# Output-projection weights ahead of the residual stream, its scaling on ScalarE, and modulation tiles spread 3, 2, 3, 2, 3, 2, 1, 0 over the mix stage of a hybrid mLSTM/Fourier diffusion step

## What is computed

```python
mod = silu(c) @ w_mod + b_mod                 # 6 x 1024 per token group
sh1, sc1, g1, sh2, sc2, g2 = split(mod, 6)
h = x * (1 + sc1) + sh1
...
merged = sigmoid(ga) * y_a + sigmoid(gb) * y_b
out = merged @ w_out
x = layer_norm(ALPHA * x + g1 * out, ln_gain[0], ln_bias[0])
h2 = x * (1 + sc2) + sh2
a, u = split(h2 @ w_ffn_in, 2)
f = (silu(a) * u) @ w_ffn_out
x = layer_norm(ALPHA * x + g2 * f, ln_gain[1], ln_bias[1])
```

## Time and profile before

| | |
|---|---|
| median of 3 runs | 1492.03 us (1490.08 to 1495.1) |
| the profiled execution | 1492.6 us, its span 1490.8 us |
| mean granted TensorE clock | 0.987 of full speed |
| PE busy | 1420.3 us (95%) |
| DVE busy | 886.2 us (59%) |
| POOL busy | 807.2 us (54%) |
| ACT busy | 329.6 us (22%) |

### The profile page before, as it was taken

The page is one execution under the profiler, slowest core; times in us unless marked ns, Lnnn a source line. Parts: engine busy times, 40 slices in busy tenths (PEclk is TensorE's granted clock), DMA queues, the critical chain, the costliest instruction groups (busy, mean ns, idle before and its releaser), DMA issues. The chain is left out here.

```text
span 1490.8 us, 24040 instructions
## 1 busy us (share of the span) xinstructions
PE 1420.3 (95%) x9397; PEld 1390.5 (93%) x9397; DVE 886.2 (59%) x1306; ACT 329.6 (22%) x563; POOL 807.2 (54%) x352
## 2 busy tenths in 40 slices
PE   5999989999999999999999999899999999999993
PEld 5999988999989989989999999899999999999993
DVE  7576786246626724753673889878997665611114
ACT  4452322221122122122233000232221111100002
POOL 1165566642463354255246777566767766756552
PEclk9999999999999999999999999899999999999997
DMA  8524244321421331132055445222223222241211
GB/s 330 193 95 146 89 168 168 104 71 61 134 73 47 99 105 57 51 134 80 31 187 203 144 167 209 91 71 69 71 70 141 70 73 82 70 177 64 78 63 70
DMA packets 57236, 164.29 MB, mean 110 GB/s; under 512 B 6072, under 2 KB 20544, under 8 KB 55880
## 3 DMA queue, kind: packets, MB, share of 16 engines
q1 hardware_dynamic: 40760, 150.87, 29.3%
q10 hardware_dynamic: 16400, 12.30, 2.5%
HBM read 145.81 MB, written 17.33 MB: 109 GB/s over the span
## 5 line engine op out<-in xcount | busy, mean ns | idle before, releaser
L676 POOL TENSOR_TENSOR w_hi<-raw,zero 128x1024 fp32r<-128x1024 f32 x156 | 313.8, 2012 | 590.9 <-PE psum L753 448.2
L680 POOL TENSOR_TENSOR w_lo<-raw,w_hi 128x1024 fp32r<-128x1024 f32 x164 | 436.6, 2662 | 38.9 <-ACT w_hi L1248 26.6
L753 PE MATMUL psum<-h_hi,w_hi 128*128 128x256 f32 (+1 forms) x768 | 177.8, 313 | 11.7 <-POOL w_lo L680 11.3
L753 PE MATMUL psum<-h_lo,w_hi 128*128 128x256 f32 (+1 forms) x768 | 176.2, 311 | 0.0
L753 PE MATMUL psum<-h_hi,w_lo 128*128 128x256 f32 (+1 forms) x768 | 176.0, 310 | 0.0
L753 PE MATMUL psum<-g_hi,w_hi 128*128 128x256 f32 x704 | 161.9, 311 | 3.4 <-DVE ta L2021 3.4
L753 PE MATMUL psum<-g_lo,w_hi 128*128 128x256 f32 x704 | 160.9, 310 | 0.0
L753 PE MATMUL psum<-g_hi,w_lo 128*128 128x256 f32 x704 | 160.6, 309 | 0.0
L753 PEld LDWEIGHTS psum<-h_hi,w_hi 128*128 128x128 f32 x768 | 139.2, 190 | 14.6 <-issue 14.0
L753 PEld LDWEIGHTS psum<-h_lo,w_hi 128*128 128x128 f32 x768 | 141.3, 190 | 0.0
L753 PEld LDWEIGHTS psum<-h_hi,w_lo 128*128 128x128 f32 x768 | 140.9, 189 | 0.0
(11 more groups left out here) (312 smaller groups left out, 3108.0 us busy)
## 6 DMA issues: line engine op xcount, KB each, us to landing
raw<-in_wunits SPq DMA_DIRECT2D x164, 512.0 KB, 3.3
mod_slot<-in_wmod SPq DMA_DIRECT2D x16, 512.0 KB, 14.0
z_ring<-in_wmod SPq DMA_DIRECT2D x16, 512.0 KB, 4.2
mod_ring<-in_wmod SPq DMA_DIRECT2D x16, 512.0 KB, 3.3
yg_dram<-yg_sb ACTq DMA_DIRECT2D x20, 256.0 KB, 2.5
yg_st<-yg_dram SPq DMA_DIRECT2D x16, 320.0 KB, 3.5
c_raw<-in_stateC SPq DMA_DIRECT2D x4, 1028.0 KB, 6.7
raw<-in_wunits SPq DMA_DIRECT2D x8, 384.0 KB, 3.1
```

Source lines behind the costliest of these rows:

```text
L676: pool.tensor_tensor(hi, src, zero[:, 0:1].broadcast_to([P, src.shape[1]]), ALU.add)\
L680: pool.tensor_tensor(lo, src, hi.bitcast(F32), ALU.subtract).then_inc(w_split, 1)
L753: ins = mm(out[:, a:z], w[:, slot, cols], x[:, k, a:z], start=(start and n == 0), stop=(stop and n == 2))
```

## The change

Three edits:

1. `MIX_MODS` gives the steps 3, 2, 3, 2, 3, 2, 1 and 0 tiles in place of 2 each.
2. SP issues out unit 2 ahead of the two DMAs of the residual stream, not behind them.
3. The stream is scaled by ALPHA on ScalarE, behind the rounding of `aug` and ahead of ScalarE's loop. VectorE waits for the first part (`aug_hi_ok >= 2`) before its loop, and for the second (`aug_hi_ok >= 3`) at the end of each round of it.

```diff
-MIX_MODS = (16, 18, 20, 22, 24, 26, 28, 30, 32)
+MIX_MODS = (16, 19, 21, 24, 26, 29, 31, 32, 32)
...
+            weights_next(U_OUT + 2)
             sp.wait_ge(units_done, U_OUT)
             for n, part in enumerate((slice(0, 2), slice(2, KD))):
                 sp.dma_start(r_all[:, part, :], xT[:, part, :]).then_inc(xf_in[n], 16)
-            for n in range(KD):
+            for n in range(1, KD):
                 weights_next(U_OUT + 2 + n)
...
             A_(g_hi[:, :, NT:NX], aug[:], ACT.Copy).then_inc(aug_hi_ok, 1)
+            for n, part in enumerate((slice(0, 2), slice(2, KD))):
+                act.wait_ge(xf_in[n], 48)
+                A_(r_all[:, part, :], r_all[:, part, :], ACT.Copy, scale=ALPHA).then_inc(aug_hi_ok, 1)
...
-            for n, part in enumerate((slice(0, 2), slice(2, KD))):
-                v.wait_ge(xf_in[n], 48)
-                own(v.tensor_scalar(r_all[:, part, :], r_all[:, part, :], ALPHA, None, ALU.mult))
+            v.wait_ge(aug_hi_ok, 2)
             with v.Fori(0, KD // 2) as i:
...
+                v.wait_ge(aug_hi_ok, 3)
```

## The result

| | before | after |
|---|---|---|
| median (range, runs) | 1491.16 us (1490.08 to 1495.1, 4) | 1512.74 us (1511.19 to 1513.59, 4) |
| profiled execution, its span | 1492.6, 1490.8 us | 1513.59, 1511.8 us |
| granted TensorE clock | 0.987 | 0.982 |

The ratio is 1.0143, with a 95% interval of 1.0131 to 1.0155. The change makes the kernel slower, as forecast, but by twice the amount: 1512.7 lies above the range of 1497 to 1510.

A forecast was written before the change was run, and what follows sets the result against it. The prediction took PE, busy for 95% of the span, to bound the kernel, so its pauses count. 1492.6 - 10.7 (handover and mix unit 10) + 21.1 (three three-tile steps) = 1503.0 us, range 1497 to 1510.

The forecast's parts named there:

- Part 1: Handover to output stage: out unit 2 issued ahead of the stream is split by 936, before PE wants it at 937.08.
- Part 2: Handover: scaling on ScalarE and no tiles in step 7 let the 10.0 us pause go; gain with mix unit 10, 10.7 us.
- the 0.7 us at mix unit 10: Mix stage: PE's 0.7 us wait for this late unit counted as gained, since SP fetches it no longer behind a tile.
- Close, but covered: Output stage: VectorE's next residual, near 941.4, is done by 942.5, where PE wants it at 944.1; 1.6 us of margin.
- Part 3: Mix steps 0, 2 and 4: SP's ring wait for the third tile delays weight units; 3 x 7.0 = 21.1 us lost.
- the same train of three: Mix stage: a tile, `z_st` and mix unit 4 issued at the earlier trace's spacing, so the unit lands 5.3 us later.
- rival C: Mix stage: the late unit's split collides with VectorE in each of three steps: +5.5, 1508.5 us; chance 0.11.
- Rival A: Mix stage: SP isn't held, mix unit 4 is in time and only the gain is left: 1481.9 us; chance 0.05.
- B (full clock): Mix stage: the pauses come but the clock stays up: +4.6, 1497.2 us; chance 0.06.
- D (handover not cleared): Handover: ScalarE's second part or the split makes PE wait at out unit 2 or 3: 1513.0 us at worst; chance 0.06.
- it lands 5.3 us later: Mix stage: mix unit 4, issued at 832.65, lands at 837.95, giving PE a pause of 5.1 us.

The follow-up runs named there:

- Scaling in pieces: Changed kernel, with ScalarE scaling channel tiles 2 to 7 in three pieces inside its loop instead of one pass ahead of it: 1509.33 us, ratio 1.0126.
- tile 0 ahead of the pass: Changed kernel, with ScalarE's second scaling still one pass but behind tile 0's square, `g_f` and `g_hi`: 1505.96 us, ratio 1.0096.
- the stream edits alone: Changed kernel with the old table of two tiles a step, keeping out unit 2 ahead and scaling on ScalarE: 1492.04 us, ratio 1.0008.
- the third tile late: Changed kernel, with SP asking for the third tile only behind the next round's weight units: 1499.03 us, ratio 1.0053.
- table alone: Kernel before with only the new table 3, 2, 3, 2, 3, 2, 1, 0: 1513.39 us, ratio 1.0151.
- The experiment with `z_st` moved: Changed kernel, with `z_st` asked for between the two weight units, not ahead of both: 1507.4 us, ratio 1.0093.
- The tiles ahead with one pass: Kernel before, two tiles a step ahead of each merge, requested between weight units, plus the change's stream edits: 1486.46 us, again 1482.85 us.
- the tiles ahead with nothing else: Kernel before, two tiles a step ahead of each merge, requested between weight units, without stream edits: 1487.75 us, ratio 0.9975.

## Why the prediction was right and wrong

**Part 1, right.** Out unit 2 is split when PE leaves out unit 0 (its `w_hi` starts at 957.89, 7.3 us after the output stage's start), and PE never waits for it.

**Part 2, the gain came, its cover failed.** The output stage is 9.2 us shorter where 10.0 were forecast, the 0.7 us at mix unit 10 are gone. The step that failed is "Close, but covered; if this cover fails, out unit 3 waits by the shortfall". I looked only at the first residual that could be late. It was: forecast at 941.4, that is 18.4 us after the output stage's start, measured at 19.8. ScalarE's pass even ended 0.9 us earlier than forecast, 14.2 us after that start; but `g_lo`, for which I had left 0.8 us, took 3.02 beside POOL's split. (`sum_1` took 3.05, which cost nothing: VectorE stood idle for 2.51 us behind it.) PE did not wait for this residual. But a VectorE that is late by some 5 us meets POOL's `w_hi` and `w_lo` with two operations a round, 2.40 and 3.01 us, instead of one (3.02, and 0.81 for the other). Its round is then 7.24 us against PE's 7.04, so it stays late, costs 0.8 us on the way, and the debt falls due at the first FFN product: 2.6 us. Scaling in pieces and tile 0 ahead of the pass each take this away. The Trainium skill's page "SBUF — State Buffer", section "Who interferes with whom", says that a VectorE instruction with two SBUF inputs contends with a GpSimd instruction that reads SBUF. The rows agree: in the output stage `sum_2` and `g_lo`, which have two such inputs, come in at 0.8 us or at 2.0 to 3.0, and the residual, which reads PSUM and one SBUF tile, at 1.0 always.

**Part 3, right in its mechanism and wrong in its price.** The path was the forecast one, row by row: tile 18 behind tile 16's end, `z_st` and the unit after it, POOL idle for the DMA (10.45 us), PE's pause, the half rate. Each pause was to be 5.1 us with 1.9 of restart. The first, against that working:

| term | forecast | measured |
|---|---|---|
| landing of the unit | 5.3 | 6.2 |
| `w_hi` | 1.89 | 2.19 |
| `w_lo` | 2.87 | 2.80 |
| starts and handovers between | 0.2 | 0.4 |
| less, from the unit's issue to PE's need | 5.15 | 5.08 |
| pause | 5.1 | 6.5 |
| restart | 1.9 | 2.2 |

The restart is worked out as there: three blocks of six matmuls take 1.73, 1.60 and 1.49 us from one to the next, where 0.88 is the full rate. The three pauses sum to 19.9 us and their restarts (2.2, 2.3, 2.4) to 6.8: 26.7 us, or 8.9 a step where I had 7.0. Less the 0.7 gained that is 26.0 of the mix stage's 26.6. Most of the other 0.6 is in how idle time is read: from the last pair before the pause to the first behind it are 6.97 us, and 6.97 - 0.29 = 6.68 are lost where the row says 6.50, so 0.2 a pause.

The term that was sized wrong most is the landing. I took "the same train of three" of the earlier trace rows (a tile, `z_st` and a unit, issued 0.4 to 0.5 us apart), and it wasn't the same: SP held at the ring is late for both slots of `raw`, so two units leave together with tile 19 behind. Without a second unit behind it, a unit third in a train at this spacing landed after 5.3 to 5.5 us in seven of eight cases (the traces of before, of the stream edits alone and of the third tile late), with one behind it after 6.0 to 6.8 in 13 of 14 (after, table alone, pieces, tile 0 first, third tile late). In the third tile late no tile follows closely, only the second unit, and the landings are 6.4 and 6.0. The exceptions are 7.2 and 5.4, so the second unit isn't the whole cause, and no run keeps it back by itself. The 7.2 was in the trace of before: it is mix unit 10, issued at 867.02 with a tile and `z_st` 0.9 and 0.5 us ahead. I used its wait as a gain and left its landing out of the range of the loss. The experiment with `z_st` moved shows that the order of these transfers matters too, by 1.2 to 2.5 us a pause.

Second is the split: I set rival C aside because VectorE's tiles "are over by 837.9, just before unit 4 lands". They are over in time (838.8, with the 1 us by which all is later). But the merge of step 1 follows them at once, and the split runs beside it: `w_hi` takes 0.3 us more at the first late unit, 0.6 at the second (2.49) and 0.15 at the third (2.04). So C is there in a small way, by another operation than the one I named.

**Sum.** From the forecast 1503.0 to the profiled execution's 1513.6 us there are 10.6: 6.2 in the mix stage (26.6 against 21.1 - 0.7), 0.8 in the output stage, 2.6 at the first FFN product and 1.0 of scatter ahead of the mix stage. Rival A (SP not held), B (full clock) and D (handover not cleared) didn't happen, though D's 1513.0 is near the result for other reasons. So two steps failed. The first is "it lands 5.3 us later" in Part 3: 6.2 to 6.6 came, so that the pauses were 6.5 to 6.7 us and not 5.1. That is 4.6 us in the three, of which 3.1 are the landing; their restarts add 1.1 and the way of reading 0.5. The second is the cover of Part 2, 3.4 us. The top of the range was rival C, a slower split and restart. A landing over 5.3 us had no term in it, and the loss behind the handover stood only in D, outside the range.

**Left open.** What decides between the on-time and the late VectorE in executions of the same program wasn't pinned down beyond its margin: `sum_2` of tile 0 starts 14.3 us after the output stage's start with the third tile behind the weights, and VectorE catches up there; at 14.9 after the change it doesn't. The tiles ahead with one pass were on time at 14.7, with a wait of PE of 2.2 us ahead of it, and late at 14.8. Also open is why two traces with the same three pauses lose 26.6 us (after) and 25.1 (in pieces) in the mix stage: the restarts differ, 6.8 us against 5.4 in all.

## What to carry to other kernels

Where one engine's queue is written out by hand, price an added request by what stands behind its wait, and look at the whole burst that leaves when the wait ends: everything held back travels together, and a unit in it lands later than it would alone (mix unit 4: 3.2 us from its issue before, 6.2 after). An engine that is "close, but covered" in the first round of a loop needs its period worked out in the late position as well, with the collisions that it then has; if that period is longer than that of its partner, the debt is never paid back and falls due at the loop's end. Spreading work unevenly to empty one step cost 27 us to gain 10; doing the same work ahead of each step's merge gained 9 to 10 and cost nothing.

## What the runs showed of the hardware

- VectorE operations on 128x16 elements took 1.74 and 2.20 us beside POOL's splits, and 0.17 without. They ended at 938.42 and 940.86, POOL's operations at 938.38 and 940.84: a tiny operation was held until the other engine's was over.
- Two engines that hold each other up can fall into a stable pattern: VectorE's round of 7.24 us kept itself for six rounds after the change, and the tiles ahead with one pass were profiled once with rounds of 7.24 and once with 7.04.
- After a pause of 3.3 us (the tiles ahead with nothing else) PE came back at 1.2 GHz, with blocks of six matmuls 1.76 and 1.44 us apart; after one of 2.2 us, in the first run of the tiles ahead with one pass, at full rate (0.99, then 0.89). But a pause of 2.1 us near 225 us of the changed kernel's span was followed by 1.35, 1.60 and 1.31, so the length of the pause alone doesn't decide.
